# Moving second-token chunks behind the first queries, and updating the first tokens by column halves

## What is computed

```python
for l in range(DEPTH):                                   # DEPTH = 2
    sh1, sc1, g1, sh2, sc2, g2 = split(silu(c) @ ada_w[l] + ada_b[l], 6)
    h = rms_norm(x, norm_mix_g[l]) * (1.0 + sc1) + sh1
    z = h @ w_in[l]                                      # 11 sections of 1024 columns
    A, Pl, R = diff_attention(z), pool(z), hgrn2(z)      # 8 heads, 4 groups, 8 heads
    x = x + g1 * ((sig(gA)*A + sig(gP)*Pl + sig(gR)*R) @ w_out[l])
    h = rms_norm(x, norm_ffn_g[l]) * (1.0 + sc2) + sh2
    q = h @ w_query[l]                                   # 8 heads, two halves of 128
    # per token and head: top 16 of 128 keys in each half, top 16 of their 256 sums,
    # softmax gate; gather u and v rows of these 16 experts
    x = x + g2 * sum_k(gate_k * gelu(u_k . h) * v_k)
out = rms_norm(x, final_g)
```

## Time and profile before

| | us |
|---|---|
| median of 3 runs | 2214.12 |
| lowest and highest run | 2212.04, 2214.23 |
| the profiled execution's own time | 2212.44 |
| its span in the profile | 2210.7 |
| TensorE busy | 1906.9 (86% of the span) |
| VectorE busy | 1478.3 (67%) |
| ScalarE busy | 674.6 (31%) |
| GpSimd busy | 610.7 (28%) |
| transfers, mean over the span | 323 GB/s |

### The profile page before, as it was taken

One profiled execution on the slowest core, in us unless ns is written; L12 is line 12 of the kernel. 1 busy time (PEld: TensorE's weight loads), 2 busy tenths in 40 slices (PEclk: granted clock), 3 DMA queues, 4 the chain that ended last, 5 costly groups with the idle time before them and its releaser, 6 DMA issues.

```text
span 2210.7 us, 22036 instructions
## 1 busy us (share of the span) xinstructions
PE 1906.9 (86%) x6452; PEld 1116.2 (50%) x6452; DVE 1478.3 (67%) x4012; ACT 674.6 (31%) x1867; POOL 610.7 (28%) x588
## 2 busy tenths in 40 slices
PE   3999999979778888877779999998889779889776
PEld 3677777644334434433257777775434334334332
DVE  5676676676766766767545676666676676776774
ACT  1222232223333333333212232231333333333331
POOL 3000000035344444444300000002345434444342
PEclk9999999989999999999989999999899999999989
DMA  9565446289999999999963335524999999999995
GB/s 377 197 237 218 169 170 237 98 336 423 421 422 421 421 422 421 421 417 421 412 250 153 150 149 201 207 103 186 391 421 421 421 421 421 422 421 421 421 415 244
DMA packets 116344, 713.03 MB, mean 323 GB/s; under 512 B 12816, under 2 KB 17168, under 8 KB 48656
## 3 DMA queue, kind: packets, MB, share of 16 engines
q0 software_dynamic: 73728, 536.90, 58.6%
q1 hardware_dynamic: 42512, 174.97, 21.0%
HBM read 710.78 MB, written 1.05 MB: 322 GB/s over the span
## 4 chain that ended last, share of the span: by engine, by line
PE 49%; DMA 26%; DVE 13%; issue 3%; POOL 2%; ACT 2%; SPq 2%; another core or an unknown queue 0%; DVEq 0%; POOLq 0%; ACTq 0%
DMA wall<-in_peer_uv,idx 24%; PE PS L1017 13%; PE PS L777 10%; PE PS L782 9%; DVE wall L1058 5%; PE PS L787 4%; PE PS L991 3%; POOL wall L551 2%; PE PS L822 2%; DMA braw<-in_ada_rows 2%; PE PS L797 1%; SPq L388 1%; PE PS L967 1%; ACT M L712 1%; DVE pos L1497 1%
## 5 line engine op out<-in xcount | busy, mean ns | idle before, releaser
L1017 PE MATMUL PS<-wall,M 128*128 128x512 f32 x2048 | 965.5, 621 | 223.6 <-ACT M L712 223.2
L1058 DVE CUSTOM_DVE_ANT_0 wall<-wall,tok 128x1024 f32<-128x1024 f32 x512 | 604.7, 1223 | 367.9 <-DMA wall<-in_peer_uv,idx 367.8
L1017 PEld LDWEIGHTS PS<-wall,M 128*128 128x128 f32 x2048 | 390.0, 198 | 763.6 <-issue 421.2
L551 POOL DMA_INDIRECT wall<-in_peer_uv,idx x512 | 565.6, 1105 | 734.2 <-PE PS L1017 342.1
L698 ACT ACTIVATE dg<-dg 128x2 f32<-128x2 f32 x256 | 52.0, 203 | 769.4 <-DVE dg L1058 769.3
L777 PE MATMUL PS<-hT,wall 128*128 128x256 f32 x1120 | 247.9, 380 | 1.8 <-DMA wall<-in_w_in 1.8
L510 POOL TENSOR_SCALAR rsb<-ms 128x4 f32<-128x4 f32 (+2 forms) x23 | 5.4, 235 | 834.5 <-DVE ms L1058 834.2
L777 PEld LDWEIGHTS PS<-hT,wall 128*128 128x128 f32 x1120 | 211.6, 190 | 32.0 <-issue 2.2
L782 PE MATMUL PS<-wall,hT 128*128 128x512 f32 x512 | 224.7, 592 | 0.0
L712 ACT ACTIVATE M<-ident,wgt 128x128 f32<-128x128 f32 x512 | 177.5, 394 | 24.3 <-ACT wgt L705 0.7
L782 PEld LDWEIGHTS PS<-wall,hT 128*128 128x128 f32 x512 | 96.2, 190 | 108.9 <-issue 108.1
(11 more groups left out here) (240 smaller groups left out, 1843.0 us busy)
## 6 DMA issues: line engine op xcount, KB each, us to landing
wall<-in_w_in SPq DMA_DIRECT2D x128, 704.0 KB, 11.7
braw<-in_ada_rows SPq DMA_DIRECT2D x80, 512.0 KB, 4.4
wall<-in_w_out SPq DMA_DIRECT2D x2, 4096.0 KB, 15.1
wall<-in_peer_uv,idx POOLq DMA_INDIRECT x512
wall<-in_ada_rows SPq DMA_DIRECT2D x6, 1024.0 KB, 12.3
mix<-in_peer_w_query SPq DMA_DIRECT2D x6, 1024.0 KB, 6.8
braw<-in_peer_w_query SPq DMA_DIRECT2D x4, 1024.0 KB, 14.2
ring<-in_peer_w_query SPq DMA_DIRECT2D x4, 1024.0 KB, 5.7
```

The source lines that it names most:

```text
L551: nc.gpsimd.indirect_dma_start(out=pair_rows[b][s], out_offset=None, in_=uv_rows, in_offset=bass.IndirectOffsetOnAxis(ap=idx[i % 2][:, k:k ...
L1017: ins = mm(bank(B_ACC + 2 * t + hf), diag[:, b, s, :], pair_rows[b][s][:, D + hf * 512:D + (hf + 1) * 512], start=(i == FIRST_TILE[t] and ...
L1058: return v.tensor_tensor_reduce(out=o, in0=a, in1=b, scale=1.0, scalar=0.0, op0=ALU.mult, op1=ALU.add, accum_out=acc)
```

## The change

On VectorE, `add_mixed(0)` and `normed(.., 0)` are replaced by `update_first`. It multiplies and adds the first tokens' update one half of the columns at a time. The squares of the left half go to ScalarE (`left_sq`, summed into `ms[:, 0:1]`), those of the right half stay on VectorE (`ms[:, 1:2]`). The norm's multiplication by the scale row comes before the root is there, and one instruction for each half is left behind it. GpSimd adds the two sums in place of the one scaling. On TensorE, the chunks of the second tokens that stood among the first tokens' last ones move: four (0 to 3) stand before `turn_state(0)`, one (4) between it and the first queries, and eleven behind the first scores.

```diff
@@ GpSimd
-                rsqrt(NR * l + HEADS + 1, 1, D, 0)
+                pool.wait_ge(s_left_ms, l + 1)
+                pool.wait_ge(s_ms, NR * l + HEADS + 2)
+                apart(pool)
+                pc(nc.gpsimd.tensor_scalar(rsb[:, 0:1], ms[:, 1:2], ms[:, 0:1], EPS, ALU.add, ALU.add))
+                pc.sync()
+                nc.gpsimd.tensor_tensor(rs[:, 0:1], rsb[:, 0:1], mhalf[:, 0:1], ALU.pow).then_inc(s_rs, 1)
@@ ScalarE, copies of chunks 6 and 7
                 for i, (k, c0, n) in enumerate(((KC - 2, 0, T), (KC - 1, 0, P), (KC - 1, P, P))):
                     act.wait_ge(s_tp, NTP * l + 8 + i)
                     nc.scalar.activation(hT[:, k, c0:c0 + n], bank(B_TURN[i])[:, c0:c0 + n], ACT.Copy).then_inc(s_hTa, 1)
+                    if i == 1:
+                        act.wait_ge(s_left, l + 1)
+                        nc.scalar.activation(left_sq, xs[:, 0, 0:512], ACT.Square, scale=1.0 / math.sqrt(D),
+                                             accum_out=ms[:, 0:1]).then_inc(s_left_ms, 1)
@@ TensorE, end of last_step
-                    out_proj(1, 0, (0,))
+                    pe.wait_ge(s_seven, l + 1)
+                    turn_chunk(KC - 1, 0).then_inc(s_tp, 1)
                     pe.wait_ge(s_hTa, NHTA * l + 6)
                     for hf in range(2):
                         out_proj(0, hf, (KC - 2,))
-                    pe.wait_ge(s_seven, l + 1)
-                    turn_chunk(KC - 1, 0).then_inc(s_tp, 1)
+                        pe.wait_ge(s_hTa, NHTA * l + 7)
+                        out_proj(0, hf, (KC - 1,)).then_inc(s_wod, 1)
                     pe.wait_ge(s_mix, mixed(l) + HEADS)
                     turn_chunk(KC - 1, 1).then_inc(s_tp, 1)
-                    out_proj(1, 0, (1,))
-                    pe.wait_ge(s_hTa, NHTA * l + 7)
-                    for hf in range(2):
-                        out_proj(0, hf, (KC - 1,)).then_inc(s_wod, 1)
@@ TensorE, behind last_step
-                out_proj(1, 0, range(2, 7))
-                pe.wait_ge(s_hTa, NHTA * l + 8)
-                out_proj(1, 0, (7,)).then_inc(s_wod, 1)
-                out_proj(1, 1, (0,))
+                out_proj(1, 0, range(4))
...
                 turn_state(0)
+                out_proj(1, 0, (4,))
                 pe.wait_ge(s_r[1], 32 * l + 16)
                 half_queries(0, 0).then_inc(s_q0, 1)
...
-                out_proj(1, 1, range(1, KC)).then_inc(s_wod, 1)
+                pe.wait_ge(s_hTa, NHTA * l + 8)
+                out_proj(1, 0, range(5, KC)).then_inc(s_wod, 1)
+                out_proj(1, 1, range(KC)).then_inc(s_wod, 1)
@@ VectorE
-                add_mixed(0)
-                normed(NR * l + HEADS + 1, 0)
+                def update_first():
+
+                    for hf in range(2):
+                        c = slice(hf * 512, (hf + 1) * 512)
+                        dve.wait_ge(s_wod, 4 * l + hf + 1)
+                        ch(v.tensor_tensor(tok[:, 0, c], bank(B_WO[0][hf]), ada[:, 0, c], ALU.mult))
+                        ch.sync()
+                        i = v.tensor_tensor(xs[:, 0, c], xs[:, 0, c], tok[:, 0, c], ALU.add)
+                        if hf == 0:
+                            i.then_inc(s_left, 1)
+                    ch(i)
+                    ch.sync()
+                    v.tensor_tensor_reduce(out=tok[:, 0, 512:D], in0=xs[:, 0, 512:D], in1=xs[:, 0, 512:D], scale=1.0 / D, scalar=0.0,
+                                           op0=ALU.mult, op1=ALU.add, accum_out=ms[:, 1:2]).then_inc(s_ms, 1)
+                    dve.wait_ge(s_left, l + 1)
+                    dve.wait_ge(s_ms, NR * l + HEADS + 2)
+                    for hf in range(2):
+                        c = slice(hf * 512, (hf + 1) * 512)
+                        ch(v.tensor_tensor(tok[:, 0, c], xs[:, 0, c], ada[:, 2, c], ALU.mult))
+                    ch.sync()
+                    dve.wait_ge(s_rs, NR * l + HEADS + 2)
+                    for hf in range(2):
+                        c = slice(hf * 512, (hf + 1) * 512)
+                        stt(tok[:, 0, c], tok[:, 0, c], rs[:, 0:1], ada[:, 1, c], ALU.mult, ALU.add).then_inc(s_tok, 1)
+
+                update_first()
```

More of the change, by code:

```diff
@@ L186, in build @@
         diag = M[:, 0:NBUF * GROUP * P].rearrange("p (b s n) -> p b s n", b=NBUF, s=GROUP)
+        left_sq = M[:, 0:512]
         qT = [M[:, o:o + 512].rearrange("p (a t) -> p a t", a=2) for o in (2048, 1536)]
@@ L303, in build @@
         s_tok = sem("s_tok")
+        s_left, s_left_ms = sem("s_left"), sem("s_left_ms")
         s_tp = sem("s_tp")
```

## The result

The changed kernel takes 2220.32 us (median of 14 runs, 2214.39 to 2225.31), the kernel before 2214.73 (14 runs, 2212.04 to 2217.54). The ratio is 1.0026, with a 95% interval of [1.0019, 1.0033]: 5.6 us slower, clear of no difference, and above the predicted range of 2205.0 to 2216.5.

The account below looks back on a forecast made before the run. Expert gathers' transfers hold the largest share, restarting after a chain that hangs on each layer's first scores; scores 1.94 us earlier in two layers give 3.9 us off 2214.12: 2210.2 us, whole range 2205.0 to 2216.5.

Parts of the forecast that it names:

- the late signal: VectorE's copy of the gate rows, delayed 5.9 and 4.8 us during the gathers, moves with the scores: no change.
- the prediction's own signs of being wrong: Gate-row copy moves differently from the scores, clock falls before the scores, or scores move under 1.6 or over 2.5 us.
- The rival that counted the delay from TensorE's work: Behind the scores TensorE ends 2.6 us later, all landing on VectorE in both layers: 5.2 on, 2215.4; chance 0.17.
- Scores' advance: First scores in each layer come 2.80 - 0.86 = 1.94 us earlier, bounds 1.6 and 2.5.
- The terms up to the mean squares: Layer 0: left half multiplied from 427.15, right half from 428.87, mean squares at 431.05, 2.2 us earlier.
- ScalarE's squares: Left half's squares take some 0.8 us, hidden under VectorE's right half; a table load of about 1.28 would still fit.
- The root: GpSimd's root beside VectorE's two multiplications ends 0.5 us later than they do; norm starts 432.9, bounds 432.39 and 433.2.
- Chunk 4's 0.86: A moved second-token chunk between transposes and first queries on TensorE adds 0.86 us, at least 0.7 on the path.
- The half-clock rival: TensorE's short waits halve its clock on the first queries: 4.6 us a layer, 2219.4 in all; chance 0.08.
- Nothing behind the scores: Eleven second-token chunks (9.5 us) behind the first scores instead of seven (6.0) stay hidden, with 3 us to spare.
- the rival's remark that TensorE's idle stretch costs: After TensorE's idle stretch its clock is 0.50; the first of the second queries take 5.00 us where 3.59 is normal.
- The gain rival: The late signal gets shorter or TensorE keeps its clock: together up to 4.9 us more gain, 2205.3; chance 0.25.

Follow-up runs that it names:

- e15: Changed kernel unedited, traced again on the chip of e13, in another session: 2215.64 us in one run, kernel before beside it 2210.11.
- the holds: ScalarE's copy of head 1's queries (changed kernel, e8) or VectorE's gate-row copy (kernel before) held until GpSimd's second root: ratios 1.0049, 0.9986, 1.0007.
- e9: Changed kernel with ScalarE's copy of head 1's first queries held until GpSimd's second root: 2222.31 us, ratio 1.0049 to the kernel before.
- e11: e8 with ScalarE's copy of head 1's queries held until GpSimd's second root: 2206.93 us, ratio 0.9986 to the kernel before.
- e6: Changed kernel unedited, measured again in a later session: 2208.27 us, ratio 0.9989 to the kernel before.
- e7: Changed kernel with chunk 4 put back ahead of the transposes, so five chunks stand there: 2208.50 us, ratio 0.9990 to the kernel before.
- e4: Changed kernel with GpSimd's first gather held until the second gate's rows are made: 2229.74 us in one run.
- e17: Changed kernel unedited, on another chip than e13 and e15: 2208.50 us in one run, kernel before beside it 2210.90.
- e8: Changed kernel with five chunks ahead of the transposes (e7) and gate rows right behind the first scores (e3): 2206.75 us, ratio 0.9983 to the kernel before.
- e18: e8 unedited, run again on the chip of e17: 2206.71 us in one run, kernel before beside it 2210.90.
- e12: Changed kernel with VectorE's two multiplications moved behind its wait for the root: 2205.86 us in one run.
- e5: Kernel before, unedited, traced again in a later session: 2209.57 us in one run.
- e1: Changed kernel with TensorE's old order, keeping VectorE's halves, ScalarE's squares and early multiplications: 2212.39 us, ratio 1.0003 to the kernel before.
- e16: e4's edit (no gather until the gate rows are made), same session and chip as e15: 2228.87 us in one run, kernel before beside it 2210.11.
- e3: Changed kernel with TensorE's gate rows moved from behind head 1's scores to just behind head 0's: 2208.21 us, ratio 0.9989 to the kernel before.
- e13: Changed kernel unedited, on the chip later used for e15: 2202.66 us in one run, kernel before beside it 2211.92.
- e2: Kernel before with TensorE's new order alone, old update and norm kept: 2212.23 us, ratio 1.0009 to the kernel before.

## Why the prediction was wrong

**The step that failed** is the one on the late signal: "As the gathers move with the scores, I take it to move with them: no change". The first half holds roughly: in the recorded pair the late signal is acted on some 14 us behind the first gather in either kernel (14.4 and 15.8 us before, 13.7 and 14.3 after; e15 has 11.4 and 14.1). But I took the late signal to be the gate rows' alone, the last on TensorE. The new order puts eleven chunks where seven stood, so head 1's queries end not 10.3 but 13.7 us behind the scores. Before, that was 4.5 us into the burst, and their end was seen on time in layer 0 and 1.2 us late in layer 1; now it is 8 us into it, and their end is what comes late. Queued behind that wait are ScalarE's copy and then, on TensorE, head 1's scores and the gate rows, both at half clock after 6 us of idleness, 4.6 and 4.4 us in place of 2.5. All that, formerly over before the late arrival, now comes after it. The copy moves by 4.40 and 3.36 us: 7.8 us where I priced nothing. Less the gain ahead of the scores, 3.2 at most and 1.6 with half clock in one layer, that gives 4.6 to 6.2; measured 5.6. Two of the prediction's own signs of being wrong were thus there: the copy moved by another amount than the scores, and the granted clock fell before them. The 7.8 is read from one trace of each kernel; the holds show that such a wait costs what the copy moves by.

**The rival that counted the delay from TensorE's work** (5.2 us on) had the right sign and the wrong mechanism and sum: it adds the 2.6 us by which TensorE's work moves, where what counts is the length of the queue behind the late wait. e9 shows that this queue behind a held signal makes such a loss, and e11 that without the queue there is none.

**Scores' advance, forecast 1.94 (1.6 to 2.5):** 1.59 at full clock. The terms up to the mean squares are within 0.03 us. ScalarE's squares took 0.63 and 0.19 with no load of a table. The root is the mis-sized term: I took 0.5 us of disturbance, with the scalar step behind the first multiplication; the upper bound (both multiplications first, 433.2) is what happened (433.27). The rule of the Trainium skill (SBUF — State Buffer, "Who interferes with whom") agrees with this trace, 1.33 us beside two-input multiplications against 0.31 without. Chunk 4's 0.86 was right against the order of before (norm's end to scores: 4.76 before, 5.62 in e6). To move it ahead, into TensorE's wait for the norm, wins 0.50 of it (e7: 12.64 for 13.14).

**The half-clock rival (chance 0.08)** was underrated, and overpriced. In the changed order TensorE's clock fell ahead of layer 0's first queries in four of ten traces (the recorded one, e4, e9, e17: 14.79 to 14.81), never in layer 1; each time it costs 1.65 us, not 4.6, since the clock comes back within the queries. With e7's five chunks before the transposes the clock stayed whole in all four traces that have them (e7, e8, e11, e18). (e12, which makes TensorE wait 2.04 us, had the half clock in layer 1: 15.12.)

**"Nothing behind the scores"**, eleven chunks hidden with 3 us to spare, was right where signals are prompt (e6, copy 17.88 as in e5's 17.86), and so was the rival's remark that TensorE's idle stretch costs. The gain rival as a whole (no late signals, up to 4.9 us less) fits what the kernel before took in the sessions of e1 to e12: medians of 2210.58 to 2211.08 in place of 2214.73. Those were other chips, so this is no measured price. With prompt signals the changed kernel gains 2.45 us of a forecast 3.9, and of the 3.2 that the scores give, with an interval (0.4 to 4.4) that holds both.

**What stays open.** Why signals come late in some executions and not in others, on the same chip and with the same code. That they need the burst of gathers is argued and not shown: the late ones all end waits within it, but e15 against e16 does not settle it, and nothing here separates the issuing of gathers from their transfers. Nor does a place in the burst suffice, as head 1's queries show that layer 0 of before saw in time. Only one trace is on record of each kernel's 14 runs, so how many of them had late signals is not known.

**The best version** is e8: 2206.75, ratio 0.9983 [0.9974, 0.9992], faster than the kernel before in a session without late signals; against the changed kernel's 2208.27 it is ahead by less than the noise. e11 shows that it keeps this under a held signal (0.9986), where the changed kernel loses 13 us. It was not caught in a session with late signals of its own.

## What to carry to other kernels

When work moves to a later place in an engine's queue, ask which signals it pushes into a stretch where a trace already shows late ones (here the back-to-back gathers), and what is queued behind each of them; the price is that queue, made at half clock, and not the shift. Make what the critical path needs before such a stretch (here the gate rows, e3, e8 and e11). Work put beside another engine's small step gains less than its length where the two contend (0.4 of 1.3 us), and a change of 0.2% wants its two kernels measured in more than one session, and both traced more than once: here one pair of traces differed by 3.6 us ahead of the change, and by signals late by different amounts, neither of which is written in the code.

## What the runs showed of the hardware

- The end of TensorE's queries, inside GpSimd's burst of ten gathers, was acted on 3.4 to 6.2 us later in some executions (after, e15) and 0.04 us later in others (e6, e13, e17), with the same code, e13 and e15 on the same chip. In the traces with late signals 40 to 52 of the 96 landing records of the burst's first 20 us are missing.
- A GpSimd scalar step on a 128x1 tile took 1.33 us beside two back-to-back 128x512 multiplications and ended behind both, against 0.31 with VectorE idle (e12).
- The granted clock fell to half ahead of the first queries after a wait of 1.7 us (2.27 in e2) in some executions and not in others: 1.65 us of difference for the same instructions (1.53 in e2).
- ScalarE's squares of 128x512 with accumulator took 0.63 + 0.19 us, beside VectorE's 0.69 + 0.08 for the other half, and with no load of a table among exponentials and copies.
